# State-space loop: sums of turned product tiles made by TensorE in PSUM, scans that read them there, and products with C that go round the four row groups

## The chip, the core and the metric

The kernel runs on one core of a Trainium2 chip. The metric is device time in microseconds (us); lower is better. Engines are named as in the profile: PE (TensorE), DVE (VectorE), ACT (ScalarE), POOL (GpSimd) and SP, which only issues DMA.

## What is computed

One inference step of a two-layer decoder, for 256 prompt tokens and 8 x 4 sample tokens of width 2048. Layer 0 mixes tokens by a diagonal complex state-space model, layer 1 by a gated recurrence; each is followed by a layer that picks and gathers experts. The change is in layer 0, in this part:

```python
def s5_mixer(h, h0_re, h0_im, lam_re, lam_im, log_dt, b_re, b_im, c_re, c_im, d_skip, w_glu, b_glu):
    u = hf.reshape(bsz, t, S5_GROUPS, S5_GROUP)          # 128 groups of 16 channels, 64 states each
    ab_re, ab_im, bb_re, bb_im = s5_discretize(...)
    bu_re = jnp.einsum("btgc,gpc->btgp", u, bb_re)
    bu_im = jnp.einsum("btgc,gpc->btgp", u, bb_im)
    ...
    _, _, s_re, s_im = lax.associative_scan(_s5_combine, (a_re, a_im, bu_re, bu_im), axis=1)
    y = (jnp.einsum("btgp,gcp->btgc", s_re, c_re) - jnp.einsum("btgp,gcp->btgc", s_im, c_im))
    y = y.reshape(bsz, t, D_MODEL) + d_skip * hf
    y = jax.nn.gelu(y, approximate=False)
```

## The kernel before

The program is written by hand for each engine; semaphores alone order the engines, and each engine runs its instructions in the order of its own code. Everything is fp32.

The state-space loop has 16 tiles k of 128 channels (8 groups). The 512 states of a tile lie as 128 partitions x 4 blocks q, so a tile of products is 128 x 1024. The complex scan is made real: the inputs are turned back by the angle that each step would add (tables COS and SIN), two real scans with the decay `dec` follow, and the results are turned forward again in the products with C.

- **PE**, `s5_in_part(k)`: two transposes of the discretized B (L757), then the products with B for the prompt (L765, 128x512, PSUM banks 0 to 3) and for the samples (L767, bank 6). `s5_out_part(k)`: the skip term (L778, L780), then for each of the four row groups q of 32 output rows four products with C for the prompt (L786, bank 5) and two for the samples (L788, bank 7). PE does `s5_in_part(k+1)`, then `s5_out_part(k)`.
- **DVE**, `s5_tile(k)`: the fraction of the angles of tile k+1 (L1258), the final states of tile k-1 (L1297, L1298), four turning products that read PSUM (L1272 to L1275), the add and subtract (L1277, L1278), eight scans (L1282), and four products that turn forward (L1288 to L1291) into `PR`, which the products with C read.
- **ACT**, `s5_tile(k)`: the tables of tile k+1 (L896 to L900, after the fraction), a copy of the samples' inputs out of PSUM (L931), the spreading of u (L911), the copy of the transposed B (L920), the angles of tile k+2 (L889, L890), the Gelu of tile k-1's output (L904, L905).
- **POOL**, `s5_tile(k)`: the discretized B of tile k+1 (L458 to L464), the four steps of the sample states (L479 to L486, once L931 is done), their copy (L495), the diagonal of the skip weights (L446).

Semaphores that the steps below touch: `s5_bu` (products with B done), `s5_bur` (DVE has read banks 0 to 3; PE's next products with B wait for it), `s5_bsc` (L931 done), `s5_bsd` (sample states done; the output part on PE waits), `s5_p` (forward products done), `s5_y` (output part done; DVE's next L1288 waits, since `PR` is one buffer), `s5_yg` (Gelu done).

A matmul of the program shows as two MATMUL rows and two LDWEIGHTS rows in the trace; a transpose as one.

Of the kernel before, what the change touches and what calls it, by code (L numbers as in the profile page):

```python
# [15 lines left out]
ALU = mybir.AluOpType  # L16
# [178 lines left out]
def hybrid_step(nc, x, norms, slabs, keys, chan, s5_vec, s5_bc, s5_h0, lru_in, u0, v0, u1, v1,  # L195
                y_out, ys_out, s5p_out, s5s_out, lru_out):
    experts_u, experts_v = [u0, u1], [v0, v1]
    with ExitStack() as ctx:
# [49 lines left out]
        vecs = view(21888, 192)  # L248

# [85 lines left out]
        s5_sf, stores = sem("s5_sf"), sem("stores")  # L335
        y_stored, pool_go = sem("y_stored"), sem("pool_go")
# [83 lines left out]
        def _(pool):  # L420
            st = Steps()
            nc.gpsimd.memset(ident[:], 0.0).then_inc(pstep, 1)
            nc.gpsimd.memset(repsum[:], 0.0).then_inc(pstep, 1)
            nc.gpsimd.memset(zeros[:], 0.0).then_inc(pstep, 1)
# [4 lines left out]
            for _ in range(5):  # L429
                st.next()  # L430
            pool.wait_ge(pstep, st.next())
            nc.gpsimd.affine_select(out=ident[:], in_=ident[:], compare_op=ALU.not_equal, fill=1.0, base=0,
                                    pattern=[[-1, P]], channel_multiplier=1).then_inc(consts, 1)
            for c in range(-COPIES + 1, COPIES):

                nc.gpsimd.affine_select(out=repsum[:], in_=repsum[:], compare_op=ALU.not_equal, fill=1.0,
                                        base=-NS * c, pattern=[[-1, P]], channel_multiplier=1).then_inc(pstep, 1)
                pool.wait_ge(pstep, st.next())
# [127 lines left out]
        def _(pe):  # L566
# [204 lines left out]
            def s5_out_part(k, h):  # L771
# [10 lines left out]
                for q in range(QK):  # L782
                    rows = slice(QC * q, QC * (q + 1))
                    cr, ci = BC[:, h, 2, rows], CN[:, h, rows]
                    for n, c in enumerate((cr, cr, ci, ci)):
                        nc.tensor.matmul(ps[rows, 5, 0:SEQ], c, PR[n][:, q, :], start=False, stop=(n == 3), skip_group_check=True)  # L786
                    for n, c in enumerate((cr, ci)):
# [4 lines left out]
            s5_in_part(0, 0)  # L792
            s5_in_part(0, 1)
            s5_out_part(0, 0)
            with pe.Fori(1, KT // 2) as i:
                for h in range(2):
                    s5_in_part(i, h)
                    s5_out_part(2 * i + (h - 1), 1 - h)
            s5_out_part(KT - 1, 1)
# [367 lines left out]
        def _(dve):  # L1167
# [92 lines left out]
            def s5_tile(i, h, first=False, last=False):  # L1260
                k = 2 * i + h
                if not last:
                    fractions(k + 1)
                if not first:
                    final_states(k - 1)
# [5 lines left out]

                V.tensor_tensor(M[0], re, cos, ALU.mult)  # L1272
                V.tensor_tensor(M[1], im, sin, ALU.mult)
                V.tensor_tensor(M[2], im, cos, ALU.mult)
                V.tensor_tensor(M[3], re, sin, ALU.mult).then_inc(s5_bur, 1)  # L1275
                dve.wait_ge(s5_bur, k + 1)
                V.tensor_tensor(M[0], M[0], M[1], ALU.add)  # L1277
                settle(V.tensor_tensor(M[2], M[2], M[3], ALU.subtract))  # L1278

                for src, dst in ((M[0], M[1]), (M[2], M[3])):  # L1280
# [3 lines left out]
                settle(ins)  # L1284
# [3 lines left out]
                V.tensor_tensor(PR[0], cos, M[1], ALU.mult)  # L1288
                V.scalar_tensor_tensor(PR[1], sin, -1.0, M[3], ALU.mult, ALU.mult)
                V.tensor_tensor(PR[2], sin, M[1], ALU.mult)  # L1290
                V.tensor_tensor(PR[3], cos, M[3], ALU.mult).then_inc(s5_p, 1)  # L1291
# [14 lines left out]
            with dve.Fori(1, KT // 2 - 1) as i:  # L1306
                st.enter(i - 1, 4)
                s5_tile(i, 0)
                s5_tile(i, 1)
            st.leave(KT // 2 - 2)  # L1310
# [374 lines left out]
```

## Time and profile before

| | |
|---|---|
| runs before (3) | 3836.89 us median, 3833.35 to 3837.49 |
| profiled execution | 3828.97 us, its span 3827.2 us |
| busy in the span | PE 77%, DVE 63%, POOL 52%, ACT 17% |
| mean granted clock of PE | 0.898 |
| state-space loop | 44.25 us (first turning product) to 363.41 us (first product of the next stage) |

The span reaches from the first to the last instruction of one execution. The page of the profile gives shares over the whole of it. Most of it is the expert layers, where DMA and PE work; the loop of this change is a twelfth, so its rows are read with a window.

### The profile page before, as it was taken

To read this page: it belongs to the slowest core of one execution; us is meant where nothing else is said; L and a number is where in the kernel's file an instruction comes from. 1 tells how busy PE (TensorE), PEld (TensorE's weight loads), DVE (VectorE), ACT (ScalarE), POOL (GpSimd) and SP (SyncE) were. 2 spreads that over 40 slices of the span, in tenths; PEclk is the share of its full clock that TensorE was granted. 3 is DMA by queue.
4 is the path that set the end of the run, shared out by engine and by line. 5 is a ranking of instruction groups with operands and counts; after the bars stand their busy time and mean duration, and the time that the engine had idled before them with its cause. 6 is when DMAs were issued, how large, how long until landed. Compare 5 with 4: busy or idle time off the path is not lost.

```text
span 3827.2 us, 30093 instructions
## 1 busy us (share of the span) xinstructions
PE 2933.0 (77%) x10500; PEld 1678.2 (44%) x10500; DVE 2398.0 (63%) x3321; ACT 654.8 (17%) x1587; POOL 1981.8 (52%) x1620
## 2 busy tenths in 40 slices
PE   5778985777666778888987789888877787666667
PEld 2334762433222325665654447655644342222222
DVE  7996047766776546666556576765456666555553
ACT  6663121011000101122010012221010111000000
POOL 5886005665665544443555553444445555555562
PEclk8888997998888999999998889999988899888888
DMA  1002339999999999999999999999999999999998
GB/s 64 11 14 88 134 137 402 420 422 423 425 424 422 427 427 427 417 415 419 420 427 423 427 422 421 424 422 422 427 427 418 420 405 427 427 427 427 427 427 319
DMA packets 197779, 1406.91 MB, mean 368 GB/s; under 512 B 21984, under 2 KB 26336, under 8 KB 26864
## 3 DMA queue, kind: packets, MB, share of 16 engines
q0 software_dynamic: 166064, 1208.62, 75.5%
q1 hardware_dynamic: 31296, 196.39, 12.5%
q8 instruction: 78, 1.28, 0.1%
q14 instruction: 53, 0.43, 0.0%
q10 hardware_dynamic: 288, 0.18, 0.0%
HBM read 1401.86 MB, written 3.24 MB: 367 GB/s over the span
## 4 chain that ended last, share of the span: by engine, by line
DMA 42%; PE 24%; POOL 14%; DVE 12%; issue 6%; ACT 2%; POOLq 0%; ACTq 0%; DVEq 0%
DMA arena<-in_v_dram,arena 27%; PE ps L663 15%; DMA arena<-in_u_dram,arena 12%; PE ps L610 7%; POOL arena L551 5%; POOL arena L540 4%; DMA W<-in_slabs_dram 3%; DVE arena L1407 3%; POOL arena L480 1%; POOL arena L482 1%; DVE X L1435 1%; POOL arena L486 1%; PE ps L675 1%; DVE arena L1340 1%; DVE arena L1333 1%
## 5 line engine op out<-in xcount | busy, mean ns | idle before, releaser
L663 PE MATMUL ps<-arena 128*128 128x512 f32 x3584 | 1798.3, 658 | 681.9 <-DMA arena<-in_v_dram,arena 523.3
L1407 DVE CUSTOM_DVE_ANT_0 arena<-arena,HN 128x2048 f32<-128x2048 f32 x576 | 1311.3, 2291 | 1080.0 <-DMA arena<-in_u_dram,arena 1079.2
L551 POOL DMA_INDIRECT arena<-in_v_dram,arena x576 | 879.9, 1528 | 1194.9 <-PE ps L663 833.2
L663 PEld LDWEIGHTS ps<-arena 128*128 128x128 f32 x3584 | 731.6, 211 | 1715.3 <-issue 948.2
L540 POOL DMA_INDIRECT arena<-in_u_dram,arena x576 | 827.1, 1436 | 547.6 <-DVE arena L1400 203.5
L610 PE MATMUL ps<-HT,W 128*128 128x160 f32 (+2 forms) x3584 | 531.0, 310 | 36.6 <-DMA W<-in_slabs_dram 32.4
L610 PEld LDWEIGHTS ps<-HT,W 128*128 128x128 f32 x3584 | 495.0, 196 | 82.2 <-DMA W<-in_slabs_dram 37.5
L1016 ACT ACTIVATE arena<-arena 128x4 f32<-128x4 f32 x144 | 29.6, 205 | 2067.7 <-DVE arena L1407 2067.7
L1435 DVE SCALAR_TENSOR_TENSOR X<-arena,X 128x2048 f32<-128x2048 f32 x128 | 301.1, 2352 | 68.7 <-DMA arena<-in_v_dram,arena 39.2
L610 PE MATMUL ps<-arena,W 128*128 128x288 f32 (+2 forms) x1536 | 257.8, 330 | 11.5 <-DMA W<-in_slabs_dram 11.0
L610 PEld LDWEIGHTS ps<-arena,W 128*128 128x128 f32 x1536 | 228.6, 194 | 44.0 <-DMA W<-in_slabs_dram 12.7
L786 PE MATMUL ps<-HN,arena 128*32 128x256 f32 x512 | 144.1, 450 | 0.0
L1025 ACT ACTIVATE arena<-ident,arena 128x128 f32<-128x128 f32 x384 | 124.7, 388 | 21.6 <-PE ps L663 21.6
L1322 DVE TENSOR_TENSOR arena<-arena 128x288 f32 x16 | 7.3, 458 | 128.5 <-ACT arena L974 128.5
L1282 DVE TENSOR_TENSOR_SCAN arena<-arena 128x256 f32<-128x256 f32 x128 | 84.0, 724 | 2.1 <-DVE arena L1278 1.9
L786 PEld LDWEIGHTS ps<-HN,arena 128*32 128x32 f32 x512 | 59.3, 127 | 56.1 <-issue 27.0
L765 PE MATMUL ps<-arena 128*128 128x512 f32 x128 | 65.6, 637 | 13.5 <-ACT arena L920 8.8
L778 PE MATMUL ps<-HT,arena 128*128 (+1 forms) x32 | 17.8, 656 | 71.1 <-POOL arena L486 58.9
L996 ACT ACTIVATE arena<-ps 128x288 f32<-128x288 f32 (+2 forms) x48 | 15.9, 331 | 238.3 <-PE ps L610 238.3
L580 PE MATMUL ps<-ident,HN 128*128 128x128 f32 (+1 forms) x192 | 28.0, 297 | 33.0 <-DVE HN L1187 21.9
L479 POOL TENSOR_TENSOR arena<-arena 128x64 f32<-128x64 f32 (+1 forms) x64 | 38.8, 606 | 25.2 <-ACT arena L931 11.4
L675 PE MATMUL ps<-HN,W 128*128 128x160 f32 (+1 forms) x256 | 41.8, 313 | 11.4 <-ACT HN L1083 11.3
(216 smaller groups left out, 1870.0 us busy)
## 6 DMA issues: line engine op xcount, KB each, us to landing
W<-in_slabs_dram SPq DMA_DIRECT2D x168, 1024.0 KB, 9.9
arena<-in_u_dram,arena POOLq DMA_INDIRECT x576, 15.3
arena<-in_v_dram,arena POOLq DMA_INDIRECT x576, 14.1
GB<-in_norms_dram SPq DMA_DIRECT2D x7, 1024.0 KB, 14.6
arena<-in_s_bc_dram SPq DMA_DIRECT2D x32, 128.0 KB, 2.1
X<-in_x_dram SPq DMA_DIRECT2D x3, 1024.0 KB, 7.1
GB<-in_keys_dram SPq DMA_DIRECT2D x2, 1024.0 KB, 13.6
out_y_dram<-HN SPq DMA_DIRECT2D x2, 1024.0 KB, 10.7
```

Source lines behind the costliest of these rows:

```text
L479: nc.gpsimd.tensor_tensor(t[0], ar, s, ALU.mult)
L540: pool.indirect_dma_start(ring[:, r, :], None, experts_u[n // LAYER_ROUNDS], bass.IndirectOffsetOnAxis(ap=GI[:, at:at + 1], axis=0)).then_ ...
L551: pool.indirect_dma_start(ring[:, HALF + r, :], None, experts_v[n // LAYER_ROUNDS], bass.IndirectOffsetOnAxis(ap=GI[:, at:at + 1], axis=0) ...
L610: mm = nc.tensor.matmul(ps[:, bank, 0:width], W[:, slot, P * k:P * (k + 1)], rhs(k), start=(k == 0), stop=(k == KT - 1))
L663: mm = nc.tensor.matmul(ps[:, ACC_BANK + c, :], diag[:, slot, :], ring[:, HALF + r, BANK * c:BANK * (c + 1)], start=first and r == 0, stop ...
L675: mm = nc.tensor.matmul(ps[:, bank, 0:CHUNK[c]], W[:, slot, at:at + P], XC[c][:, 2 * (b // 4) + e, :], start=(e == 0), stop=(e == 1))
L765: nc.tensor.matmul(ps[:, 2 * c + e, :], BT[:, c, :], UX[:, 2 * e:2 * e + 2, NS:NT], start=True, stop=True)
L786: nc.tensor.matmul(ps[rows, 5, 0:SEQ], c, PR[n][:, q, :], start=False, stop=(n == 3), skip_group_check=True)
L1025: A(diag[:, m % DIAGS, :], (ident if tile_of(n) < 2 else repsum)[:], ACT.Copy, scale=WG[:, at:at + 1]).then_inc(diag_set, 1)
L1282: ins = V.tensor_tensor_scan(dst[:, q, :], dec[:, bass.ds(k * QK + q, 1)].to_broadcast([P, SEQ]), src[:, q, :], 0.0, ALU.mult, ALU.add)
L1407: V.tensor_tensor_reduce(ring[:, r, :], ring[:, r, :], HN[:, tile_of(n), :], 1.0, 0.0, ALU.mult, ALU.add, A8[:, n % TURN, r:r + 1]).then_i ...
L1435: V.scalar_tensor_tensor(X[:, t, :], ring[:, HALF + r, :], WG[:, at:at + 1], X[:, t, :], ALU.mult, ALU.add).then_inc(add_done, 1)
```

## The change

- PE gets `s5_sums(k)`: for the real and the imaginary part it multiplies the two turned product tiles with the identity, or with the negative identity, and adds them in banks 0 to 3, in place of the products with B that DVE has read by then. A new constant `negative` is made by POOL.
- DVE's add and subtract go. The scans read PSUM and write M[0] and M[2]. The fraction and the final states move from ahead of the turning products to behind them. `s5_bur` is given after the scans, no longer after the turning products.
- The output part is cut in two: `s5_out_first` (skip term, and the products with C of PR[0] and PR[1]) and `s5_out_rest` (PR[2], PR[3] and the samples). The inner loop now runs over the row groups.

```diff
+            def s5_sums(k):
+
+                for c in range(2):
+                    pe.wait_ge(s5_turned, 2 * k + (c + 1))
+                    for e in range(2):
+                        nc.tensor.matmul(ps[:, 2 * c + e, :], ident[:], M[2 * c][:, 2 * e:2 * e + 2, :], start=True, stop=False)
+                        mm = nc.tensor.matmul(ps[:, 2 * c + e, :], negative if c else ident[:],
+                                              M[2 * c + 1][:, 2 * e:2 * e + 2, :], start=False, stop=True)
+                    mm.then_inc(s5_sum, 1)
+
+            def s5_out_first(k, h):
...
+                y_products(h, (0, 1))
+
+            def y_products(h, parts):
+
+                for n in parts:
+                    for q in range(QK):
+                        rows = slice(QC * q, QC * (q + 1))
+                        c = BC[:, h, 2, rows] if n < 2 else CN[:, h, rows]
+                        mm = nc.tensor.matmul(ps[rows, 5, 0:SEQ], c, PR[n][:, q, :], start=False, stop=(n == 3),
+                                              skip_group_check=True)
+                return mm
+
+            def s5_out_rest(h):
+
+                y_products(h, (2, 3))
...
             with pe.Fori(1, KT // 2) as i:
                 for h in range(2):
                     s5_in_part(i, h)
-                    s5_out_part(2 * i + (h - 1), 1 - h)
-            s5_out_part(KT - 1, 1)
+                    s5_out_first(2 * i + (h - 1), 1 - h)
+                    s5_sums(2 * i + h)
+                    s5_out_rest(1 - h)
+            s5_out_first(KT - 1, 1)
+            s5_out_rest(1)
...
             def s5_tile(i, h, first=False, last=False):
                 k = 2 * i + h
-                if not last:
-                    fractions(k + 1)
-                if not first:
-                    final_states(k - 1)
                 dve.wait_ge(s5_bu, k + 1)
                 dve.wait_ge(s5_tab, k + 1)
...
+                V.tensor_tensor(M[3], re, sin, ALU.mult)
+                if not first:
+                    dve.wait_ge(s5_p, k)
                 V.tensor_tensor(M[0], re, cos, ALU.mult)
-                V.tensor_tensor(M[1], im, sin, ALU.mult)
-                V.tensor_tensor(M[2], im, cos, ALU.mult)
-                V.tensor_tensor(M[3], re, sin, ALU.mult).then_inc(s5_bur, 1)
-                dve.wait_ge(s5_bur, k + 1)
-                V.tensor_tensor(M[0], M[0], M[1], ALU.add)
-                settle(V.tensor_tensor(M[2], M[2], M[3], ALU.subtract))
-
-                for src, dst in ((M[0], M[1]), (M[2], M[3])):
+                V.tensor_tensor(M[1], im, sin, ALU.mult).then_inc(s5_turned, 1)
+                V.tensor_tensor(M[2], im, cos, ALU.mult).then_inc(s5_turned, 1)
+                if not last:
+                    fractions(k + 1)
+                if not first:
+                    final_states(k - 1)
+
+                for c, (src, dst) in enumerate(((re, M[0]), (im, M[2]))):
+                    dve.wait_ge(s5_sum, 2 * k + (c + 1))
                     for q in range(QK):
                         ins = V.tensor_tensor_scan(dst[:, q, :], dec[:, bass.ds(k * QK + q, 1)].to_broadcast([P, SEQ]),
                                                    src[:, q, :], 0.0, ALU.mult, ALU.add)
-                settle(ins)
+                ins.then_inc(s5_bur, 1)
+                dve.wait_ge(s5_bur, k + 1)
```

The order on PE in the body of its loop, one tile, before: the products with B of tile k+1, then the output part of tile k. The rows of the program count matmuls once; ISA and REGISTER_ALU rows are address and wait steps.

```order
L765 MATMUL ps<-arena 128x512 [waits s5_bur,s5_bsc,s5_ux,s5_btc]
L765 MATMUL ps<-arena 128x512
L767 MATMUL ps<-arena 128x128
L765 MATMUL ps<-arena 128x512 x2
L767 MATMUL ps<-arena 128x128
L777 REGISTER_ALU [waits s5_p,s5_bsd,s5_cn,s5_dd]
L778 ISA [waits s5_yg]
L778 MATMUL ps<-HT,arena 128x256
L780 ISA
L780 MATMUL ps<-HT,arena 128x32
L786 MATMUL ps<-HN,arena 32x256 x4
L788 MATMUL ps<-arena 32x32 x2
```

The last two rows stand four times, once for each row group. The same place of the change, from the end of the products with B on:

```order
L793 REGISTER_ALU [waits s5_p,s5_bsd,s5_cn,s5_dd]
L794 ISA [waits s5_yg]
L794 MATMUL ps<-HT,arena 128x256
L796 ISA
L796 MATMUL ps<-HT,arena 128x32
L806 MATMUL ps<-HN,arena 32x256 x8
L780 ISA
L782 MATMUL ps<-arena,ident 128x512 [waits s5_turned]
L783 MATMUL ps<-arena,ident 128x512
L782 MATMUL ps<-arena,ident 128x512
L783 MATMUL ps<-arena,ident 128x512
L780 REGISTER_ALU
```

Behind it come the second half of the sums, again behind a wait for `s5_turned`, then eight L806 and eight L817. So the sums of tile k+1 stand behind the skip term and half of the products with C of tile k, which wait for the sample states of tile k.

The order on DVE in one tile, before:

```order
L1258 SCALAR_TENSOR_TENSOR arena<-HN,arena 128x1024 [waits s5_prod]
L1297 ISA [waits s5_p]
L1297 TENSOR_TENSOR arena<-HN 128x4
L1298 ISA
L1298 TENSOR_TENSOR arena<-HN 128x4
L1272 TENSOR_TENSOR arena<-ps,arena 128x1024 [waits s5_tab,s5_bu]
L1273 TENSOR_TENSOR arena<-ps,arena 128x1024
L1274 TENSOR_TENSOR arena<-ps,arena 128x1024
L1275 TENSOR_TENSOR arena<-ps,arena 128x1024
L1277 TENSOR_TENSOR arena<-arena 128x1024 [waits s5_bur]
L1278 TENSOR_TENSOR arena<-arena 128x1024
```

The same place of the change, where the scans print as SCALAR_TENSOR_TENSOR, as they do before:

```order
L1303 TENSOR_TENSOR arena<-ps,arena 128x1024 [waits s5_tab,s5_bu]
L1306 TENSOR_TENSOR arena<-ps,arena 128x1024 [waits s5_p]
L1307 TENSOR_TENSOR arena<-ps,arena 128x1024
L1308 TENSOR_TENSOR arena<-ps,arena 128x1024
L1292 REGISTER_ALU
L1293 SCALAR_TENSOR_TENSOR arena<-HN,arena 128x1024 [waits s5_prod]
L1333 ISA [waits s5_p]
L1333 TENSOR_TENSOR arena<-HN 128x4
L1334 ISA
L1334 TENSOR_TENSOR arena<-HN 128x4
L1315 ISA
L1317 ISA [waits s5_sum]
```

The fraction (now L1293) has moved behind the four turning products, the add and subtract are gone, and the scans (L1317) wait for PE's sums.

## Rows read from the trace of the kernel before

**Rows 1.** The page of the profile, its first line.
```profile
span 3827.2 us, 30093 instructions
```

**Rows 2.** DVE's timeline (start us, us, what), tiles 0 and 13; then busy times between them.
```profile
44.25 1.23 DVE L1272 TENSOR_TENSOR arena<-ps,arena 128x1024 f32<-128x1024 f32 x1 [1.78 <-PE ps L767]
...
296.48 1.21 DVE L1272 TENSOR_TENSOR arena<-ps,arena 128x1024 f32<-128x1024 f32 x1
...
core 0: us, PE busy (x) PEld busy (x) DVE busy (x) ACT busy (x) POOL busy (x), PEclk, DMA share, GB/s
44.25:296.48 252.23, 185.61 (x806) 97.10 (x804) 246.24 (x273) 156.12 (x281) 215.78 (x351) 0.84 0.04 13
```

**Rows 3.** DVE's timeline, one tile.
```profile
159.77 1.21 DVE L1272 TENSOR_TENSOR arena<-ps,arena 128x1024 f32<-128x1024 f32 x1
...
164.41 1.28 DVE L1277 TENSOR_TENSOR arena<-arena 128x1024 f32<-128x1024 f32 x1
...
167.24 5.32 DVE L1282 TENSOR_TENSOR_SCAN arena<-arena 128x256 f32<-128x256 f32 x8 [0.16 <-DVE arena L1278]
172.59 1.23 DVE L1288 TENSOR_TENSOR HN<-arena 128x1024 f32<-128x1024 f32 x1
...
177.56 1.28 DVE L1258 SCALAR_TENSOR_TENSOR arena<-HN,arena 128x1024 f32<-128x1024 f32 x1
...
178.99 1.21 DVE L1272 TENSOR_TENSOR arena<-ps,arena 128x1024 f32<-128x1024 f32 x1
```

**Rows 4.** POOL's timeline, sample states of the same tile.
```profile
160.11 0.35 POOL L482 TENSOR_TENSOR arena<-arena 128x64 f32<-128x64 f32 x1
...
166.40 0.84 POOL L479 TENSOR_TENSOR arena<-arena 128x64 f32 x1 [0.40 <-POOL arena L464]
...
175.35 1.22 POOL L482 TENSOR_TENSOR arena<-arena 128x64 f32<-128x64 f32 x1
...
179.16 0.33 POOL L479 TENSOR_TENSOR arena<-arena 128x64 f32<-128x64 f32 x1 [0.18 <-POOL arena L486]
```

**Rows 5.** PE's timeline, the same tile; idle time and its releaser in brackets.
```profile
161.49 0.69 PE L778 MATMUL ps<-HT,arena 128*128 x2 [3.35 <-POOL arena L486]
...
162.38 3.42 PE L786 MATMUL ps<-HN,arena 128*32 128x256 f32 x8
...
171.12 0.44 PE L757 MATMUL ps<-ident,arena 128*128 128x128 f32 x2
172.03 1.98 PE L765 MATMUL ps<-arena 128*128 128x512 f32 x4 [0.47 <-ACT arena L920]
...
174.07 1.88 PE L765 MATMUL ps<-arena 128*128 128x512 f32 x4
175.79 0.38 PE L767 MATMUL ps<-arena 128*128 128x128 f32 x2
181.24 1.22 PE L778 MATMUL ps<-HT,arena 128*128 x2 [5.07 <-POOL arena L486]
```

**Rows 6.** Windows: busy times as in rows 2, the granted clock (PEclk) third from the end.
```profile
162.10:165.40 3.30, 3.30 (x11) 1.49 (x10) 3.27 (x4) 3.25 (x6) 2.96 (x7) 0.50 0.00 0
...
179.20:185.80 6.60, 4.56 (x12) 2.58 (x13) 6.57 (x6) 5.01 (x8) 5.38 (x13) 0.50 0.00 0
```

**Rows 7.** PE's timeline, seven L786 of one group and the change of groups.
```profile
165.88 1.67 PE L786 MATMUL ps<-HN,arena 128*32 128x256 f32 x7
167.39 0.19 PE L788 MATMUL ps<-arena 128*32 128x32 f32 x1
167.40 0.40 PE L786 MATMUL ps<-HN,arena 128*32 128x256 f32 x1
167.42 0.26 PE L788 MATMUL ps<-arena 128*32 128x32 f32 x3
```

**Rows 8.** ACT's timeline, the copy of the samples' inputs.
```profile
182.26 0.36 ACT L931 ACTIVATE arena<-ps 128x256 f32<-128x256 f32 x1
```

**Rows 9.** PE's timeline, the output part of the last tile and what follows it.
```profile
353.16 1.16 PE L778 MATMUL ps<-HT,arena 128*128 128x256 f32 x2 [5.30 <-DVE HN L1291]
...
363.41 1.00 PE L610 MATMUL ps<-arena,W 128*128 128x288 f32 x3 [0.56 <-ACT arena L905]
```

More of the change, by code:

```diff
@@ L248, in hybrid_step @@
         vecs = view(21888, 192)
+        negative = view(22080, P)
         SIG = view(17792, 4 * NT).rearrange("p (n m) -> p n m", n=4)
@@ L335, in hybrid_step @@
         s5_sf, stores = sem("s5_sf"), sem("stores")
+        s5_turned, s5_sum = sem("s5_turned"), sem("s5_sum")
         y_stored, pool_go = sem("y_stored"), sem("pool_go")
@@ L423, in _ @@
             nc.gpsimd.memset(repsum[:], 0.0).then_inc(pstep, 1)
+            nc.gpsimd.memset(negative, 0.0).then_inc(pstep, 1)
             nc.gpsimd.memset(zeros[:], 0.0).then_inc(pstep, 1)
@@ L428, in _ @@
                            allow_small_or_imprecise_dtypes=True).then_inc(pstep, 1)
-            for _ in range(5):
+            for _ in range(6):
                 st.next()
@@ L433, in _ @@
                                     pattern=[[-1, P]], channel_multiplier=1).then_inc(consts, 1)
+            nc.gpsimd.affine_select(out=negative, in_=negative, compare_op=ALU.not_equal, fill=-1.0, base=0,
+                                    pattern=[[-1, P]], channel_multiplier=1).then_inc(pstep, 1)
+            pool.wait_ge(pstep, st.next())
             for c in range(-COPIES + 1, COPIES):
@@ L769, in s5_in_part @@
                 mm.then_inc(s5_bu, 1)
-            def s5_out_part(k, h):
+            def s5_sums(k):
[7 more added lines that the diff above has]
+            def s5_out_first(k, h):
                 pe.wait_ge(s5_dd, k + 1)
@@ L781, in s5_out_part @@
                                  start=True, stop=False, skip_group_check=True)
[L782 to L787, printed above, removed]
+                y_products(h, (0, 1))
[9 more added lines that the diff above has]
+                y_products(h, (2, 3))
+                for n in range(2):
+                    for q in range(QK):
+                        rows = slice(QC * q, QC * (q + 1))
+                        c = CN[:, h, rows] if n else BC[:, h, 2, rows]
                         mm = nc.tensor.matmul(ps[rows, 7, 0:NS], c, BSF[:, h, n, NS * q:NS * (q + 1)], start=False,
@@ L792, in _ @@
             s5_in_part(0, 0)
+            s5_sums(0)
             s5_in_part(0, 1)
-            s5_out_part(0, 0)
+            s5_out_first(0, 0)
+            s5_sums(1)
+            s5_out_rest(0)
             with pe.Fori(1, KT // 2) as i:
@@ L1283, in s5_tile @@
                                                    src[:, q, :], 0.0, ALU.mult, ALU.add)
-                settle(ins)
+                ins.then_inc(s5_bur, 1)
+                dve.wait_ge(s5_bur, k + 1)
                 if not first:
                     dve.wait_ge(s5_y, k)
[L1288 to L1291, printed above, removed]
+                V.tensor_tensor(PR[0], cos, M[0], ALU.mult)
+                V.scalar_tensor_tensor(PR[1], sin, -1.0, M[2], ALU.mult, ALU.mult)
+                V.tensor_tensor(PR[2], sin, M[0], ALU.mult)
+                V.tensor_tensor(PR[3], cos, M[2], ALU.mult).then_inc(s5_p, 1)
             def final_states(k):
@@ L1306, in _ @@
             with dve.Fori(1, KT // 2 - 1) as i:
-                st.enter(i - 1, 4)
                 s5_tile(i, 0)
                 s5_tile(i, 1)
-            st.leave(KT // 2 - 2)
             s5_tile(KT // 2 - 1, 0)
```

## The prediction, on record before the changed kernel ran

> **What bounds it now.** I read the page first: the span is 3827.2 us [rows 1]. The change touches only the state-space loop, 16 tiles near the start, between 44.25 and 363.4 us, so the question is what one tile costs. DVE's first turning product starts at 44.25 in tile 0 and at 296.48 in tile 13 [rows 2]: 252.23 us for 13 tiles, 19.40 us each. In the same stretch DVE is busy 246.24 of 252.23 us, POOL 215.78, PE 185.61, and PE's granted clock is 0.84 [rows 2]. So DVE is all but full, but POOL is close behind it.
>
> Next, the timeline of one tile, engine by engine. Times below are counted from DVE's first turning product, here 159.77. DVE [rows 3]: four turning products 4.64 us (to 164.41); the add and the subtract with their settling 2.83 (to 167.24); eight scans 5.35 (to 172.59); four products for the output 4.97 (to 177.56); fraction and final states 1.43 (to 178.99).
>
> POOL [rows 4]: the states of the samples begin at 166.40, which is 6.63 in, and the last of them releases PE at 181.24 [rows 5], 21.47 in: 14.84 us. These are small instructions that DVE holds up: the same L482 takes 1.22 us beside a DVE product with both inputs in SBUF and 0.35 beside one that reads PSUM. A step of the four takes at most 2.08 us when free (179.16 to PE's start at 181.24).
>
> PE [rows 5]: released at 161.49, 0.89 us for the two products with the skip, then the products with C until 171.12, transposes and the wait for ACT until 172.03, the products with B until 176.17, and then nothing for 5.07 us. That idle time costs clock: after idle times of 3.35 and 5.07 us the granted clock is 0.50, which is 1.2 GHz, in 162.1 to 165.4 and 179.2 to 185.8 [rows 6]. Eight L786 instructions then take 3.42 us, 0.43 each; at full clock seven start between 165.88 and 167.40, 0.217 apart [rows 5, 7]. A matmul of the program is two instructions here.
>
> So three chains of nearly one length close the loop: DVE's own 19.2 us, POOL's samples, and samples to PE to DVE (the output products of tile k+1 wait for s5_y of tile k).
>
> **What the change removes.** The add, the subtract and their settling: 2.83 us of DVE per tile. With them two instructions go that hold POOL up. The scans now have one input in PSUM, and beside such DVE instructions POOL runs free [rows 4], so POOL gains in the scans too.
>
> **What it adds.** On PE 8 matmuls of 128x512, 16 instructions. Four L765 and two L767 stand between 172.03 and 174.07, and four L765 take 174.07 to 175.79, 0.43 each at full clock [rows 5]. So 8 x 0.43 = 3.44 us for a half of the sums, 6.9 per tile, twice that at 1.2 GHz. DVE covers some of the first half: after the third turning product (3.48) it still has the fourth (to 4.64) and fraction and states (1.43, to 6.07). Its scans can start at 3.48 + 3.44 + 0.2 for the hand-over = 7.1, a wait of 1.0; the second four at 10.6, a wait of 0.8, and end at 13.3; the output products end at 18.3. That is the best tile: 18.3 against 19.2. I keep 5.35 for the scans. No row shows a scan out of PSUM; a turning product takes 1.16 with an input there, an output product 1.24 with both in SBUF [rows 3], so 0.08 less or more for each of eight, 0.6 us per tile either way.
>
> The products of B for tile k+1 used to run during the scans. They now wait until the scans of tile k are done, since both use banks 0 to 3. They start at 13.3 and take 4.14 (172.03 to 176.17), to 17.4; the next tile's turning may start at 18.3. They are hidden by 0.9 us, and no longer so at 1.2 GHz.
>
> **The groups.** Row group by row group, 32 L786 instructions of 0.217 take 6.9 us at full clock. In round robin, neighbours use different groups. Do these overlap? At the one place where before changes groups, they do [rows 7]: an L786 of the next group starts at 167.40, between the small L788 of the old group at 167.39 and 167.42, which stand ahead of it in the program. Four full streams at once are not shown; bounds are 6.9 (none) and 1.7 (all four). I take a third, 2.3 us per tile, 1.2 for the half before the sums, nearer the overlap that is seen. The Trainium skill, page "TensorE: Matmul & The Clock Gate", section "The mechanism", says the opposite of this row on one point: that matmuls start strictly in program order. By that rule the two passes of one matmul would hold back the next group, and the half would take 1.7 instead of 1.2; this trace does not agree, with 167.40 before 167.42.
>
> **Where the stall goes.** The fraction moves behind the turning products, and this is late next. ACT makes the tables from it, and only then copies the samples' input, which POOL waits for. Today the fraction starts at 177.56 and that copy ends at 182.62 [rows 3, 8], 5.06 later. New: 4.64 + 5.06 = 9.7 in, against a start of the samples at 6.63 today. Four free steps are 8.3 us; the four output products fall among them, and let one instruction through each instead of some 12 in 5 us, which costs 3 us more. So PE is released at about 21.0, against 21.5 now. POOL wins 3.5 us and the late start takes 3 back.
>
> From there: 0.9 for the skip, 1.2 for the half of the products with C, 3.44 + 0.2 for the first half of the sums, the same for the second, 2.7 for the last scans, 4.97: 21.0 + 0.9 + 1.2 + 7.1 + 2.7 + 5.0 = 37.9 for two tiles, **18.9 each** at full clock, a good one of 18.3 and a late one of 19.6. What used to cross PE in 9.6 us (161.49 to 171.12) still crosses it in 9.2.
>
> **The clock.** In the late tile PE has nothing from 17.4 to 21.0, 3.6 us. After 3.35 and 5.07 us without work the clock fell in the trace, so I expect it to fall there, in every second tile, and not after the shorter gap of the others (18.7 to 21.0, 2.3 us). It costs 1.7 us (3.3 us of half speed from 162.1) to 2.3 (181.24 to 185.8), and now it hits the products with C and the sums, on the path. That is 2.0 in two tiles, 1.0 each: 18.9 + 1.0 = **19.9 us per tile against 19.40**.
>
> **The sum.** 14 tiles in the steady state at +0.5: +7. At the end, with nothing beside it, stands the output part of tile 15, 353.16 to 363.41 [rows 9]; its 6.9 us of products with C become 2.3: -4.6. The extra memset, the affine_select on POOL and the semaphores lie in POOL's wait ahead of the loop: 0. What follows starts when the loop ends and moves with it. Together +2.4 us. The profiled execution took 3828.97 us (1.8 around the span of 3827.2), the median of the runs is 3836.89, 7.9 above it. 3836.9 + 2.4 = **3839**. No change can be told from one below 0.2%, 7.7 us.
>
> **The rivals.**
> - *The clock holds* (0.24). The groups and the sums keep PE busy for longer, and it idles less in all: per tile 4.1 + 0.9 + 0.9 + 2.3 + 0.4 + 6.9 = 15.5 of 19. Then 18.9 per tile: 14 x -0.5 - 4.6 = -11.6, 3825. Against it: the gap of 3.6 us. It decides in favour if samples release PE within some 3 us of the end of B's products.
> - *The clock falls in every tile* (0.19), slower. If the low stretch is as long as the second of the trace (6.6 us), or comes in the good tile too, the sums, the products with B and the scans behind them all stretch: 2.0 per tile instead of 1.0 would be 20.9; DVE covers a part, so 20.4. 14 x 1.0 - 4.6 = +9.4, 3846. It decides from a gap of 3 us on in the good tile.
> - *Groups overlap two at a time* (0.08). The half takes 1.7, +0.5 in two tiles, +3.5, and the end gains 3.5 instead of 4.6: +7, 3844. The page's rule named above would give this.
> - *The groups don't overlap* (0.07), slower. PE is then the bound: 4.1 + 0.9 + 0.9 + 6.9 + 0.4 + 6.9 = 20.1, and some 1.0 of hand-overs: 21.1, 14 x 1.7 = +24, nothing at the end: 3861. Rows 7 speak against it.
>
> **How the numbers follow.** My forecast, between 3834 and 3845, has 0.42. Faster by over 0.2%: the clock that holds, and a little of the forecast if the scans are cheaper out of PSUM: 0.26. Slower by over 0.2%: the last case, most of the fall in every tile, some of the pairs and of the forecast's upper edge: 0.33. Within it: 0.41. For the range: scans 0.6 per tile cheaper at held clock would take it to about 3820, of which I leave out the last part; above I leave out the case without overlap. 3822 to 3856.
>
> **What would show it.** DVE: gaps of about 1 us ahead of the first and the fifth scan in good tiles, 3 and more ahead of the first in late ones; no POOL instruction over 0.7 us during scans; POOL's samples starting 9.7 in and taking 11 us; L806 instructions of four groups starting within some 60 ns; PEclk 0.5 in every second tile; turning products 18 to 19 and 21 us apart in turn. The forecast is wrong if the samples release PE well before the output products are done, if L806 starts stand 0.2 us apart all along, or if the mean of a tile is under 19 or over 20.5.

## The result, and the profile after

| | before | after |
|---|---|---|
| median (16 runs each) | 3835.87 us | 3844.02 us, 3836.46 to 3852.05 |
| ratio of the two | | 1.0019, 95% interval 1.0012 to 1.0026 |
| span of the profiled execution | 3827.2 us | 3841.8 us |
| first turning product to first product of the next stage | 44.25 to 363.41 us | 44.44 to 363.39 us |

The forecast was 3839, its range 3822 to 3856. The time lies in it, 5 us above the forecast. The last row of the table is the surprise: the loop, where the changed code stands, takes the same time. Against [rows 2], in the same stretch of 13 tiles (DVE's timeline, then the windows):

```profile
44.44 1.23 DVE L1303 TENSOR_TENSOR arena<-ps,arena 128x1024 f32<-128x1024 f32 x1 [11.80 <-PE ps L773]
...
44.44:299.67 255.23, 200.94 (x1014) 95.67 (x1014) 205.83 (x245) 157.68 (x281) 161.13 (x356) 0.93 0.04 13
```

255.23 us is 19.63 per tile, against 19.40. DVE's busy time fell from 246.24 to 205.83 and POOL's from 215.78 to 161.13, and no engine is full any more; the tile is now set by waits. The same tile as in [rows 3], and the start of the next, on DVE:

```profile
163.39 1.21 DVE L1303 TENSOR_TENSOR arena<-ps,arena 128x1024 f32<-128x1024 f32 x1
...
167.91 1.21 DVE L1293 SCALAR_TENSOR_TENSOR arena<-HN,arena 128x1024 f32<-128x1024 f32 x1
...
170.78 2.42 DVE L1317 TENSOR_TENSOR_SCAN arena<-arena,ps 128x256 f32<-128x256 f32 x4 [1.51 <-PE ps L783]
174.09 2.42 DVE L1317 TENSOR_TENSOR_SCAN arena<-arena,ps 128x256 f32<-128x256 f32 x4 [0.89 <-PE ps L783]
176.54 1.23 DVE L1324 TENSOR_TENSOR HN<-arena 128x1024 f32<-128x1024 f32 x1
...
181.53 1.21 DVE L1303 TENSOR_TENSOR arena<-ps,arena 128x1024 f32<-128x1024 f32 x1
```

18.14 us for this tile, with the two gaps ahead of the scans that were foretold (1.51 and 0.89). Eight scans take 2 x 2.42 instead of 5.32. PE in the same stretch, for [rows 5], and its next skip term:

```profile
163.95 0.69 PE L794 MATMUL ps<-HT,arena 128*128 x2 [1.17 <-POOL arena L492]
...
164.72 1.07 PE L806 MATMUL ps<-HN,arena 128*32 128x256 f32 x16
166.92 1.12 PE L782 MATMUL ps<-arena,ident 128*128 128x512 f32 x2 [1.13 <-DVE arena L1307]
...
176.76 1.96 PE L771 MATMUL ps<-arena 128*128 128x512 f32 x4 [1.22 <-DVE arena L1317]
...
184.22 0.69 PE L794 MATMUL ps<-HT,arena 128*128 x2 [3.34 <-POOL arena L492]
```

Sixteen L806 take 1.07 us, the time of four: the row groups overlap fully. POOL, for [rows 4]: the samples' states start once ACT's copy (L966) is done, 9.72 us into the tile, and end at 183.85, 20.46 in. In the tile of [rows 4], POOL came to the samples only 6.63 us in and waited for its own L464; nobody waited for the copy.

```profile
172.39 0.36 ACT L966 ACTIVATE arena<-ps 128x256 f32<-128x256 f32 x1
...
173.11 0.29 POOL L485 TENSOR_TENSOR arena<-arena 128x64 f32 x1 [5.64 <-ACT arena L966]
...
176.39 0.26 POOL L492 TENSOR_TENSOR arena<-arena 128x32 f32<-128x32 f32 x1
176.84 1.13 POOL L485 TENSOR_TENSOR arena<-arena 128x64 f32<-128x64 f32 x1 [0.19 <-POOL arena L492]
...
183.58 0.27 POOL L492 TENSOR_TENSOR arena<-arena 128x32 f32<-128x32 f32 x1
```

Ten of them fit into 3.5 us beside the scans, the next four take 1.02 to 1.31 us each beside the output products. Where PE starts a late tile at the low clock, the sums stretch. PE in two other tiles, the first of them tile 0:

```profile
47.98 2.07 PE L782 MATMUL ps<-arena,ident 128*128 128x512 f32 x2 [3.64 <-DVE arena L1307]
49.85 1.91 PE L783 MATMUL ps<-arena,ident 128*128 128x512 f32 x2
51.56 1.83 PE L782 MATMUL ps<-arena,ident 128*128 128x512 f32 x2
...
241.29 1.22 PE L794 MATMUL ps<-HT,arena 128*128 x2 [3.32 <-POOL arena L492]
242.30 0.47 PE L796 MATMUL ps<-HT,arena 128*128 x2
242.70 1.94 PE L806 MATMUL ps<-HN,arena 128*32 128x256 f32 x16
244.57 2.08 PE L782 MATMUL ps<-arena,ident 128*128 128x512 f32 x2
```

The end of the loop, for [rows 9]:

```profile
357.56 1.19 PE L794 MATMUL ps<-HT,arena 128*128 128x256 f32 x2 [6.21 <-issue]
...
358.94 3.64 PE L806 MATMUL ps<-HN,arena 128*32 128x256 f32 x32
362.36 0.44 PE L817 MATMUL ps<-arena 128*32 128x32 f32 x16
363.39 0.85 PE L616 MATMUL ps<-arena,W 128*128 128x288 f32 x1 [0.59 <-ACT arena L940]
```

5.83 us from the skip term on, against 10.25.

### The profile page after: what moved, and what is told of

Read it like the earlier page. It is cut to its first block, busy times and chain, and to the rows that moved or that the text cites. A ratio compares the mean times of both kernels' runs of the same rounds, so it can differ in the third digit from the quotient of the medians.

```text
span 3841.8 us, 30603 instructions
## 1 busy us (share of the span) xinstructions
PE 2949.7 (77%) x10756; PEld 1675.1 (44%) x10756; DVE 2349.2 (61%) x3289; ACT 655.1 (17%) x1587; POOL 1905.0 (50%) x1622
## 3 DMA queue, kind: packets, MB, share of 16 engines
q8 instruction: 78, 1.28, 0.1%
## 4 chain that ended last, share of the span: by engine, by line
DMA 41%; PE 27%; DVE 13%; POOL 11%; issue 5%; ACT 2%; POOLq 0%; DVEq 0%; ACTq 0%
DMA arena<-in_v_dram,arena 26%; PE ps L669 15%; DMA arena<-in_u_dram,arena 11%; PE ps L616 8%; POOL arena L557 5%; POOL arena L546 5%; DMA W<-in_slabs_dram 4%; DVE arena L1441 3%; PE ps L782 1%; DVE X L1469 1%; PE ps L783 1%; PE ps L681 1%; DVE arena L1374 1%; DVE arena L1367 1%; DVE arena L1317 1%
## 5 line engine op out<-in xcount | busy, mean ns | idle before, releaser
L557 POOL DMA_INDIRECT arena<-in_v_dram,arena x576 | 863.6, 1499 | 1218.8 <-PE ps L669 881.1
L546 POOL DMA_INDIRECT arena<-in_u_dram,arena x576 | 836.7, 1453 | 541.2 <-issue 366.0
L1317 DVE TENSOR_TENSOR_SCAN arena<-arena,ps 128x256 f32<-128x256 f32 x128 | 77.4, 667 | 59.7 <-PE ps L783 59.7
L782 PE MATMUL ps<-arena,ident 128*128 128x512 f32 x128 | 73.6, 659 | 13.4 <-DVE arena L1307 13.4
L485 POOL TENSOR_TENSOR arena<-arena 128x64 f32<-128x64 f32 (+1 forms) x64 | 27.2, 425 | 91.9 <-ACT arena L966 82.7
L1441 DVE DVE_READ_ACCUMULATOR2_ANT arena<- 128x1 f32 x576 | 47.7, 83 | 0.0
L782 PEld LDWEIGHTS ps<-arena,ident 128*128 128x128 f32 x128 | 25.0, 207 | 47.2 <-issue 29.0
```

The source lines that it names most:

```text
L546: pool.indirect_dma_start(ring[:, r, :], None, experts_u[n // LAYER_ROUNDS], bass.IndirectOffsetOnAxis(ap=GI[:, at:at + 1], axis=0)).then_ ...
L557: pool.indirect_dma_start(ring[:, HALF + r, :], None, experts_v[n // LAYER_ROUNDS], bass.IndirectOffsetOnAxis(ap=GI[:, at:at + 1], axis=0) ...
L782: nc.tensor.matmul(ps[:, 2 * c + e, :], ident[:], M[2 * c][:, 2 * e:2 * e + 2, :], start=True, stop=False)
L1317: ins = V.tensor_tensor_scan(dst[:, q, :], dec[:, bass.ds(k * QK + q, 1)].to_broadcast([P, SEQ]), src[:, q, :], 0.0, ALU.mult, ALU.add)
L1441: V.tensor_tensor_reduce(ring[:, r, :], ring[:, r, :], HN[:, tile_of(n), :], 1.0, 0.0, ALU.mult, ALU.add, A8[:, n % TURN, r:r + 1]).then_i ...
```

## The experiments

Loop end is the start of the first product of the next stage in the run's one profile. "Rest" is the median less the loop end, for what stands behind it. Kernels that were timed together share their runs of before, and each ratio is to those. Before was timed four times, with medians of 3835.87 (16 runs), 3837.71 (15), 3836.41 (27) and 3836.58 (29), 3836.77 over all 87; its two profiles have loop ends of 363.41 and 366.12, so its rest is 3472.0. Two profiles of one kernel can differ by 2.7 us in loop end, so the rest is no surer than that.

| kernel | median us (runs) | ratio, 95% interval | loop end | rest |
|---|---|---|---|---|
| before_again | 3837.39 (11) | 1.0001, 0.9992 to 1.0010 | 366.12 | 3471.3 |
| rr_only | 3830.92 (11) | 0.9980, 0.9970 to 0.9991 | 359.58 | 3471.3 |
| before_early_copy | 3831.41 (11) | 0.9984, 0.9975 to 0.9993 | 359.87 | 3471.5 |
| before_padded | 3841.97 (12) | 1.0013, 1.0004 to 1.0022 | 366.01 | 3476.0 |
| the change | 3844.02 (16) | 1.0019, 1.0012 to 1.0026 | 363.39 | 3480.6 |
| after_again | 3843.39 (11) | 1.0020, 1.0011 to 1.0029 | 364.16 | 3479.2 |
| one_by_one | 3844.20 (10) | 1.0022, 1.0013 to 1.0032 | 365.75 | 3478.5 |
| filler | 3833.69 (10) | 0.9987, 0.9978 to 0.9996 | 355.31 | 3478.4 |
| early_copy | 3818.04 (5) | 0.9948, 0.9934 to 0.9962 | 344.68 | 3473.4 |
| early_copy_again | 3819.77 (6) | 0.9956, 0.9944 to 0.9968 | 345.11 | 3474.7 |
| fraction_first | 3869.66 (4) | 1.0083, 1.0068 to 1.0098 | 396.81 | 3472.9 |

**The loop alone: cut_before, cut_after.** Both kernels end with the state-space loop: the other mixer and all expert layers are left out. The loop itself is that of before and of the change.

> The kernel before, cut off behind the state-space loop: everything after the last output part of layer 0's mixer is left out (glu, experts, layer 1), and the outputs are filled with whatever stands in memory; only the state-space loop's time is read. By its trace the whole kernel reaches that point at 363.4 us, so the span is about 363 us and a few for the stores. Its time is the base for the other cut kernel.

> The changed kernel, cut at the same place, with the same work left out. Two theories for the 7.3 us (0.19%) that the change costs in the medians of the whole kernels. (A) The loop itself is slower in most executions, and the one that was profiled (loop end at 363.39 against 363.41) was a lucky one: then this kernel is some 7 us above the other cut kernel. (B) The loop takes the same time, and the loss lies behind it, in stages that the change doesn't touch: then both cut kernels are within 2 us.

375.64 us (374.94 to 377.22, 5 runs) and 375.09 (374.32 to 375.83, 5 runs). The medians lie 0.6 us apart, less than the runs of one kernel scatter, so the loop takes the same time within about 1 us (theory B). With the loop ends of the whole kernels this puts the 7 us behind the loop, where no instruction differs.

**early_copy.** The change, with ACT's copy of the samples' inputs and the spreading of u ahead of the tables:

```diff
-                if not last:
-                    if not first:
-                        act.wait_ge(s5_p, k)
-                    tables(k + 1, 1 - h)
                 act.wait_ge(s5_bu, k + 1)
...
                 if not last:
                     spread_u(k + 1)
+                    if not first:
+                        act.wait_ge(s5_p, k)
+                    tables(k + 1, 1 - h)
                     matrices(k + 1)
```

> The changed kernel, with one part moved: ACT copies the samples' inputs out of PSUM and spreads u before it makes the next tile's tables, not behind them. Theory 1 (the late tile comes from the sample states: fraction behind the turning products, tables behind the fraction, copy behind the tables, POOL 9.7 us late, PE without work for 3.3 us at low clock afterwards): POOL then starts near the tile's beginning and is done some 10 us before PE needs it, every tile takes 18.1 us, and the loop loses 14 x 1.3 = 18 us: 3826 in the medians, ratio to before 0.997 to 0.995, PEclk 1.0 nearly throughout. Rival (PE's own work and the hand-overs between DVE and PE set the late tile): POOL's release moves but tiles keep 19.4 in the mean, time as the changed kernel's, 3844.

> The change with the early copy once more, for its stages behind the loop. Theory A (programs that are made from the change lose some 5 us behind the loop): the medians give 3471 to 3476 us behind the loop, so 3820 to 3823 in all. Theory B (they don't, or not when the loop ends at another time): 3816 to 3819, ratio 0.995 as at the first time.

20 us faster than before at the first time and 17 at the second, 24 to 26 faster than the change: the fastest kernel of the study. Of the 26, 18.7 lie in the loop (363.39 to 344.68), close to the 18 that were expected; the other 7 lie behind it, where the loss of the change is nearly gone, and nothing here explains that. The second time falls at the border of its two theories and decides nothing on the stages behind the loop. POOL's first sample instruction, PE's skip term and the window over the ten steady tiles from 122.30 on:

```profile
160.58 0.29 POOL L485 TENSOR_TENSOR arena<-arena 128x64 f32 x1 [0.40 <-POOL arena L470]
```
```profile
177.06 0.69 PE L794 MATMUL ps<-HT,arena 128*128 x2 [1.04 <-ACT arena L951]
```
```profile
122.30:303.48 181.18, 145.79 (x820) 70.33 (x820) 158.44 (x192) 123.35 (x222) 120.48 (x281) 1.00 0.05 14
```

The samples start 2.04 us into their tile (from 158.54) instead of 9.72, nobody waits for them, and PE's longest idle times are 1.0 to 1.3 us. All tiles are good ones, 181.18 / 10 = 18.12, at the full clock. The late tile was the late copy. Set beside before_early_copy (below), which was timed together with early_copy_again, the rest of the change, taken together, gains 11.6 us (3831.41 against 3819.77), 14.8 in loop end, once the copy is early in both kernels.

**filler.** The change, with three products of 128x256 ahead of each skip term, whose result nobody reads:

```diff
             def s5_out_first(k, h):
 
+                for _ in range(3):
+                    nc.tensor.matmul(ps[:, 4, SEQ:2 * SEQ], ident[:], HT[:, 0, NS:NT], start=True, stop=True)
```

> The changed kernel, with three products with the identity, 128x256, into an unused part of a PSUM bank, ahead of the skip term on PE in every tile; their results are read by nobody. They take 1.3 us at full clock, in a gap of PE of 1.2 us (good tiles) to 3.3 us (late ones). Theory 1 with the clock: PE's idle time falls to about 2 us in late tiles, the clock no longer falls, and the late tile (20.5 us) loses its slow matmuls: some 1 to 1.5 us per two tiles, 7 to 10 us in all, 3835. Rival (the clock costs nothing, since DVE and POOL set the pace): no change or, by the added work in front of the sums, up to 3 us slower.

```profile
123.19:291.78 168.59, 142.27 (x794) 72.16 (x793) 144.63 (x172) 112.45 (x199) 119.33 (x255) 1.00 0.05 14
```

As expected: more work on PE made the loop 8 us shorter. The clock is full in the nine tiles of this window, 18.73 each, with the samples as late as in the change. By these windows the fallen clock costs a steady tile 0.7 us (19.4 to 18.7), and the late samples without it 0.6 (18.7 to 18.1, early_copy).

**rr_only.** Before, with only the round robin over the row groups:

```diff
-                for q in range(QK):
-                    rows = slice(QC * q, QC * (q + 1))
...
+                for n in range(4):
+                    for q in range(QK):
+                        rows = slice(QC * q, QC * (q + 1))
```

> The kernel before, with the round robin alone: its products with C go round the four row groups, and nothing else is changed. The groups overlap fully (16 L806 in 1.07 us in the changed kernel), so the output part takes 2 us instead of 9 after POOL's release. Theory (in the kernel before, DVE's own 19.2 us per tile set the pace and the output part was nearly hidden): the waits ahead of L1288 go, about 0.2 us per tile in the mean (19.40 to 19.2), and at the end of the loop 5 us: -8 us, 3828. Rival (POOL's samples are the pace, through PE): more than that, since POOL's release may now come 7 us later; but POOL runs no faster, so no more than 8 us either. If the low clock becomes more frequent, by PE's longer idle time, the products with B double, hidden by the scans.

5.5 us faster by the medians, where 8 were expected. The output part of the last tile takes 5.1 us instead of 10.25 (354.49 to 359.58): that is nearly all of it. In the steady state many tiles are 19.9, and DVE shows why (its timeline, one tile, then POOL's):

```profile
236.37 1.21 DVE L1275 TENSOR_TENSOR arena<-ps,arena 128x1024 f32<-128x1024 f32 x1
...
241.01 1.42 DVE L1280 TENSOR_TENSOR arena<-arena 128x1024 f32<-128x1024 f32 x1
242.36 1.42 DVE L1281 TENSOR_TENSOR arena<-arena 128x1024 f32<-128x1024 f32 x1
243.93 5.78 DVE L1285 TENSOR_TENSOR_SCAN arena<-arena 128x256 f32<-128x256 f32 x8 [0.16 <-DVE arena L1281]
```
```profile
241.61 3.94 POOL L458 TENSOR_TENSOR arena<-arena 128x128 f32<-128x128 f32 x4 [0.26 <-issue]
```

DVE never waits; its own instructions with all inputs in SBUF have grown: the scans from 5.32 to 5.78, the add from 1.28 to 1.42. POOL is at work for most of the tile in both kernels, but not on the same thing. In before its products of 128x128 (L458, four in 1.47 us from 162.60) run beside turning products that read PSUM; here the samples finish later, and the same L458 run beside the add and the scans and take 3.94. The starts of the scans follow it: in before they stand 0.60 to 0.72 us apart beside the samples' 128x64 and 128x32, here up to 0.80 beside the 128x128 (246.03, 246.82 and 247.62). That POOL slows DVE, as DVE slows POOL, is the reading that these rows suggest; no run takes POOL's work away. The second profile of before has such tiles too, of 20.2 and 20.3 us with scans of up to 5.64, and ends its loop 2.7 us later than the first. The tile is 19.88 (236.37 to 256.25), against 19.2 in [rows 3].

**one_by_one.** The change, without the round robin: within a half, one row group is finished before the next.

```diff
-                for n in parts:
-                    for q in range(QK):
+                for q in range(QK):
+                    for n in parts:
```

> The changed kernel, with its products with C of the prompt row group by row group again, in both halves. Nothing else is changed. The prediction's last rival: PE then needs 5.2 us more per tile (32 instructions 0.217 apart against 16 in 0.9 twice) and becomes the bound at 21 to 22 us per tile, against 19.4 to 19.6: 15 x 2 + 5 = +35 us over the changed kernel, 3879. If only the half ahead of the sums is on the path: 2.6 us in two tiles or in each, +20 to +40. Rival (late tiles hide it, since the samples set them): +10.

The expectation missed: the same time as the change. PE's timeline:

```profile
164.81 1.09 PE L806 MATMUL ps<-HN,arena 128*32 128x256 f32 x16
...
184.29 1.22 PE L794 MATMUL ps<-HT,arena 128*128 x2 [3.33 <-POOL arena L492]
```

Sixteen L806 take 1.09 us, with four of one group in a row in the program, and the first four start 0.013 us apart, at 164.810, 164.824, 164.837 and 164.850. The rows don't name the group, but a group's own instructions stand 0.217 apart, so these are of four groups. The overlap needs no round robin; it needs that a group has few instructions in a row. With the twelve of before (eight L786, four L788) PE starts the next group only when three of the old one are left [rows 7].

**fraction_first.** The change, with the fraction and the final states back ahead of the turning products:

```diff
                 k = 2 * i + h
+                if not last:
+                    fractions(k + 1)
+                if not first:
+                    final_states(k - 1)
...
                 V.tensor_tensor(M[2], im, cos, ALU.mult).then_inc(s5_turned, 1)
-                if not last:
-                    fractions(k + 1)
-                if not first:
-                    final_states(k - 1)
```

> The changed kernel, with the fraction and the final states ahead of the turning products again, as in the kernel before. The tables and the samples then start early (some 5 us in), and no tile is late for POOL; but DVE has only one turning product to do while PE makes the first half of the sums: a wait of 2.5 us in each tile, and PE's idle time sits before the output part. Theory: each tile takes 19.8 us if the clock holds, 20.5 if it falls in some: +5 to +15 us over the changed kernel, 3849 to 3859. Rival (the late samples cost more than the cover is worth): faster than the changed kernel by 5 us or more.

26 us slower than the change, more than the 5 to 15 expected; in the loop it is 33 (363.39 to 396.81), and the rest is 8 us shorter. PE, then DVE:

```profile
201.58 2.08 PE L782 MATMUL ps<-arena,ident 128*128 128x512 f32 x2 [2.98 <-DVE arena L1311]
203.45 1.91 PE L783 MATMUL ps<-arena,ident 128*128 128x512 f32 x2
205.16 1.91 PE L782 MATMUL ps<-arena,ident 128*128 128x512 f32 x2
```
```profile
208.44 2.42 DVE L1317 TENSOR_TENSOR_SCAN arena<-arena,ps 128x256 f32<-128x256 f32 x4 [5.78 <-PE ps L783]
```

The samples are early here, and so PE is done with the first half of the output part early, and waits 2.98 us for the turned tiles. The clock falls in each tile looked at (0.50 to 0.55 in windows from 180.00, 201.50 and 224.40 on), and the sums run into it with nothing on DVE to cover them: 5.78 us of wait, then 0.89. Tiles take 21.5 and 22.8 us in turn. So the move of the fraction is no side issue of the change: without that cover the sums stand in the open.

**after_again, before_again.** Both kernels unchanged.

> The changed kernel, word for word, a second time on another chip, with a second profile. The cut kernels show that the loop takes the same time in both kernels, so the 7.3 us stand behind it, in stages whose code is the same. Theory A (a real and steady effect on the stages behind): ratio again 1.001 to 1.003, and the profile again shows the expert stage of layer 0 (500 to 1320 us) some 9 us longer than before's 815 us. Theory B (it is chance in the DMA-bound stages, or a matter of the chip): ratio within 0.999 to 1.001, and the stage anywhere between 815 and 825 us.

> The kernel before, unchanged, under a label of its own: what a comparison shows where nothing differs, and a second profile of its stages behind the loop. Theory A (the 7 us that the change costs stand behind the loop and are its own): ratio 1.000 within 0.001, and the stages between 363.4 us and the end take 3464 to 3470 us in the profile, as in the first profile of before (3463.7), against 3475 to 3478 in two profiles of the change. Theory B (the first profile of before was a lucky execution, and the stages behind the loop vary by that much whatever the kernel): 3470 to 3478 here too, and the medians must then be explained by chance: ratio up to 1.0015.

The 7 us of the change are there again, and before compared with itself gives 1.0001. But the second profile of before has a span of 3838.6 us: of the 14.6 us between the first two spans, some ten were chance, as theory B had it, while the medians went as theory A had them. One profile each can't place 7 us; the medians and the cuts did. Nor do stage lengths: the first stage of experts behind the loop, 815.2 us in the first profile of before and 824.3 in that of the change, has 818.1 and 820.5 in their second ones, and 820.4 in rr_only, which loses nothing behind the loop.

**before_padded.** Before, with eight products of 128x32 ahead of each output part, as many instructions as the sums are:

```diff
             def s5_out_part(k, h):
 
+                for _ in range(8):
+                    nc.tensor.matmul(ps[:, 4, SEQ:SEQ + NS], ident[:], HT[:, 0, 0:NS], start=True, stop=True)
```

> The kernel before with 8 small products (128x32, identity times a part of HT, into columns of bank 4 that nobody reads) ahead of each output part, where PE waits for the samples anyway. PE's code for the loop is then as long as the change's, with no other part of the change. Theory L (the length or place of PE's code sets how the stages behind the loop run): loop end within 1 us of 363.4, and 4 to 7 us more behind it, 3841 to 3843 against 3836. Theory N (the code's length is nothing; it is something else of the change, or chance): within 2 us of before.

+5.4 us by the medians (1.5 to 8.4 by the interval), within the range of theory L. Its other condition, a loop end within 1 us of 363.4, is missed: the loop end is that of before_again to 0.1 us, and measured against the first profile of before, 2.6 of the 5.4 would lie in the loop. So products that nobody waits for cost some 3 to 5 us behind the loop, which speaks for theory L. The table agrees in its order: the kernels whose PE code is as long as before's have a rest of 3471.3 to 3472.0, all with longer code have more. But these reach from 3472.9 (fraction_first) to 3480.6 (the change) at one length of code, so length alone does not set it. Nor is more code loaded: the two DMA queues for instructions move 1.28 and 0.43 MB in before, in before_padded and in the change alike. What does set it is open. The first stage behind the loop is bound by DMA; windows of 700 us of it, the last column in GB/s, in before, padded and the change:

```profile
600.00:1300.00 700.00, 491.32 (x1121) 225.97 (x1122) 499.74 (x772) 68.70 (x210) 430.60 (x276) 0.86 1.01 422
```
```profile
600.00:1300.00 700.00, 484.44 (x1103) 223.24 (x1104) 497.30 (x766) 64.56 (x202) 418.83 (x275) 0.85 1.01 419
```
```profile
600.00:1300.00 700.00, 487.01 (x1102) 224.40 (x1103) 496.29 (x766) 64.53 (x202) 421.42 (x273) 0.84 1.01 418
```

In this window the queues move a little less: 3 in 420 GB/s of 700 us are 5 us. But the second profile of before has 421, after_again 420, early_copy 421, filler 421 with a rest of 3478.4, and fraction_first 417 with the smallest rest of the longer kernels, so this is a lead and no proof.

**before_early_copy.** Before, with the early copy alone.

> The kernel before with only ACT's order changed: the copy of the samples' inputs and the spreading of u stand ahead of the tables. My theory (before is bound by DVE's own 19.2 us per tile, and by POOL's samples that DVE holds up, not by the time at which they start): the samples start some 1 to 2 us sooner, the clock falls less, and a tile gains 0.2 us at most: 0 to -4 us, ratio 0.999 to 1.000. Rival (the late copy is as much a part of before's bound as of the change's): -10 us or more, ratio under 0.9975, and then the gain of the early copy says little of the change.

5.2 us faster, a little over the expectation and short of the rival's 10: in before, the late copy was nearly hidden.

## Why the prediction came out as it did

- **What bounds before.** DVE all but full, POOL close behind: borne out. Starting the samples sooner gains little there (before_early_copy, 5.2 us), and a cheaper output part gains at the end only (rr_only). DVE's own tile is no fixed 19.2 us: it depends on which of POOL's instructions run beside it, 19.2 in [rows 3] and 19.9 in rr_only.
- **The sums** cost 0.43 per instruction as worked out, start 3.53 us into the tile (forecast 3.48), and leave gaps of 1.51 and 0.89 (1.0 and 0.8).
- **The scans** were kept at 5.35; out of PSUM the eight take 4.84. This is the term of the tile that was off most: 0.5 us, near the end of its bound of 0.6. They take 2.42 for four in every tile of the change, also where POOL is at work (174.09). A good tile is 18.13 instead of 18.3.
- **The groups** overlap fully: a half costs 0.9 us (164.72 to 165.6), not 1.2, though the bound of all four at once, 1.7 for a tile, would have given it. The Trainium skill, page "TensorE: Matmul & The Clock Gate", section "The mechanism", has matmuls start strictly in program order. In one_by_one, with four of a group in a row 0.217 apart, only the first of each group could start beside the last of the one before, so sixteen would take 13 x 0.217 = 2.8 us, and the row above has 1.09; the measurement decides against it, as rows 7 did.
- **The samples** start 9.72 us in (forecast 9.7) and release PE 20.5 in (21.0). The tiles come in pairs, as forecast, but for one: behind the good tile of 181.53 come 18.94 and 20.01.
- **The clock** falls in nearly every second tile and costs 0.7 us per tile by filler, forecast 1.0. Late tiles take 20.0 to 22.2 where it fell, forecast 21.6, and 18.94 where it held. The forecast of 19.9 per tile came out at 19.43 from the third tile on, since scans, groups, release and clock are each a little cheaper. Before has 19.50 there, so this is -0.1, not +0.5. In the sum itself, 21.0 + 0.9 + 1.2 + 7.1 + 2.7 + 5.0, the two halves of the sums with their hand-over are 7.3 and not 7.1, which is 0.1 per tile.
- **The first two tiles** were summed as if they were like all others. They take 41.46 us against 37.72, +3.7: PE comes to tile 0's sums after 3.64 us without work, at the low clock. DVE of the change and of before, first turning product of tile 2:

```profile
85.90 1.21 DVE L1303 TENSOR_TENSOR arena<-ps,arena 128x1024 f32<-128x1024 f32 x1
```
```profile
81.97 1.21 DVE L1272 TENSOR_TENSOR arena<-ps,arena 128x1024 f32<-128x1024 f32 x1
```

- **The end** gains 4.4 us, forecast 4.6, by two errors that cancel: full overlap, at half the clock (32 L806 in 3.64 us, the granted clock 0.50 from 357.56 to 362.60).
- **The sum** for the loop was +2.4; it is 0, by profile and by the cuts. "What follows starts when the loop ends and moves with it" is the step that failed: 7 to 9 us came there. They are in stages that the argument took as fixed, and without them the forecast would have been some 3 us too high instead of 5 too low. That the change came out slower, as forecast, is luck: the loop, from which the forecast was added up, did not get slower, and the loss stands in a term that was put at nothing and whose cause is open. What is borne out is the account of the tile.
- **The rivals.** What the clock that holds would give is seen in filler: 18.7 per tile (18.9 was worked out for it), and 3833.7, with most of that remainder in it, where 3825 was worked out. Two groups at a time and no overlap are excluded.

## What to carry to other kernels

When two engines slow each other and a third waits for both, taking work off one makes the next late event the bound: here ACT's copy, which had been hidden, stood late once the fraction had moved behind the turning products, and was worth 19 us of loop. Look, after such a change, for the short instruction that stands behind long ones on its engine and that others wait for, and move it ahead. And measure a part by itself when the effect is under 0.3%: the spans of two executions of before differ by as much (3827.2 and 3838.6).

## What the hardware showed that I had not expected

- Scans of 128x256 with their input in PSUM start 0.58 to 0.60 us apart (2.42 for four), with POOL idle or at work. From SBUF they start 0.60 to 0.80 apart, by what POOL does beside them: 5.32 for eight beside the samples' 128x64 and 128x32, 5.78 where 128x128 come in. No row of this loop has scans from SBUF with POOL idle, so how much of the gain is PSUM's own, and how much is POOL no longer in the way, isn't shown.
- Four row groups (of 32 output rows) run at once, fp32, and their instructions don't keep to the program's order across groups: 16 instructions of 128x32 by 256 in 1.07 us, where seven of one group take 1.67 [rows 7]. In the change the first four L806 of the late tile start at 184.984, 184.990, 184.997 and 185.004. With 12 instructions of a group in a row the others wait.
- The same idle time of PE does not always lower the clock. After 3.34 us, at 184.22 in the change, it stayed at full speed, and fell after 3.32 us at 241.29 and 3.33 in one_by_one, and once after 2.53 (PE from 202.47; sixteen L806 take 1.87 there). What windows at these two places of the change show:

```profile
184.20:187.50 3.30, 3.28 (x24) 1.89 (x25) 3.30 (x5) 0.20 (x1) 3.03 (x6) 1.00 0.00 0
```
```profile
243.00:246.00 3.00, 3.00 (x18) 1.24 (x11) 1.94 (x4) 1.34 (x2) 2.71 (x5) 0.50 0.00 0
```
